# First mixer loop of a hybrid decoder step: GpSimd's state product put behind the decay tables, attention copy and tables put ahead of the gates, mLSTM gate sums in one product

## The reference

```
x = post(0, x, _swiglu(pre(0, x), ...), 0.5)     # FFN
y, st = _mix(pre(1, x), l, prm, past)            # three mixers in parallel
x = post(1, x, y, 1.0)
x = post(2, x, _swiglu(pre(2, x), ...), 0.5)     # FFN
```

## Time and profile before

| | |
|---|---|
| median of three runs | 2043.45 us (2041.63 to 2048.05) |
| profiled execution | 2043.22 us |
| its span | 2041.4 us |
| TensorE busy | 1851.3 us (91%), 12436 records |
| VectorE busy | 965.1 us (47%) |
| ScalarE busy | 720.3 us (35%) |
| GpSimd busy | 81.7 us (4%) |
| transfers | 391.48 MB, mean 192 GB/s |

### The profile page before, as it was taken

One profiled execution on the slowest core, in us unless ns is written; L12 is line 12 of the kernel. 1 busy time (PEld: TensorE's weight loads), 2 busy tenths in 40 slices (PEclk: granted clock), 3 DMA queues, 4 the chain that ended last, 5 costly groups with the idle time before them and its releaser, 6 DMA issues. The chain is left out here.

```text
span 2041.4 us, 33570 instructions
## 1 busy us (share of the span) xinstructions
PE 1851.3 (91%) x12436; PEld 1567.1 (77%) x12436; DVE 965.1 (47%) x1749; ACT 720.3 (35%) x1317; POOL 81.7 (4%) x111
## 2 busy tenths in 40 slices
PE   6999989999987897999969999899999878979997
PEld 4988966776765686998959888667767656869997
DVE  4555425335355534555355553253353644346554
ACT  3554323323321103554345443233233211046552
POOL 0000010000000001000010000100000000010001
PEclk7999989999998998999979999999999888989999
DMA  7777642462348922456547776342641588325561
GB/s 320 279 281 293 252 170 84 167 232 109 134 154 211 272 104 101 166 200 254 226 165 271 299 292 227 146 161 81 237 183 59 165 256 224 110 99 174 213 229 69
DMA packets 87842, 391.48 MB, mean 192 GB/s; under 512 B 14402, under 2 KB 19778, under 8 KB 57410
## 3 DMA queue, kind: packets, MB, share of 16 engines
q1 hardware_dynamic: 72738, 368.24, 50.8%
q10 hardware_dynamic: 15008, 21.95, 2.9%
HBM read 377.32 MB, written 12.83 MB: 191 GB/s over the span
## 5 line engine op out<-in xcount | busy, mean ns | idle before, releaser
L982 DVE TENSOR_TENSOR ring_parts<-ring,pages_parts 128x1024 fp32r<-128x1024 f32 (+1 forms) x272 | 314.3, 1191 | 199.2 <-ACT pages_parts L1539 199.1
L451 PE MATMUL ps<-xn,ring 128*128 128x264 f32 x1664 | 400.0, 401 | 6.1 <-ACT xn L1546 6.1
L490 PE MATMUL ps<-arena_parts,pages_parts 128*128 128x264 f32 x1408 | 361.4, 292 | 23.5 <-DVE xn_parts L1050 21.1
L451 PEld LDWEIGHTS ps<-xn,ring 128*128 128x128 f32 x1664 | 326.9, 199 | 70.0 <-issue 10.4
L491 PE MATMUL ps<-xn_parts,pages_parts 128*128 128x264 f32 x1408 | 357.0, 288 | 0.0
L1539 ACT ACTIVATE pages_parts<-ring 128x1024 fp32r<-128x1024 f32 (+1 forms) x272 | 267.8, 1025 | 179.8 <-DMA ring<-in_w_ffn_in 71.8
L490 PEld LDWEIGHTS ps<-arena_parts,pages_parts 128*128 128x128 f32 x1408 | 271.8, 193 | 44.2 <-issue 43.6
L491 PEld LDWEIGHTS ps<-xn_parts,pages_parts 128*128 128x128 f32 x1408 | 271.2, 193 | 0.0
L495 PE MATMUL ps<-arena_parts,ring_parts 128*128 128x264 f32 x1408 | 196.5, 283 | 0.0
L490 PE MATMUL ps<-big_parts,pages_parts 128*128 128x264 f32 x704 | 177.6, 288 | 6.6 <-DVE gates_parts L996 6.6
L495 PEld LDWEIGHTS ps<-arena_parts,ring_parts 128*128 128x128 f32 x1408 | 181.9, 188 | 0.0
(11 more groups left out here) (312 smaller groups left out, 2039.6 us busy)
## 6 DMA issues: line engine op xcount, KB each, us to landing
ring<-in_w_ffn_in SPq DMA_DIRECT2D x88, 1024.0 KB, 4.9
ring<-in_w_ada SPq DMA_DIRECT2D x32, 1536.0 KB, 6.5
ring<-in_w_a SPq DMA_DIRECT2D x32, 1536.0 KB, 11.1
ring<-in_w_ffn_down SPq DMA_DIRECT2D x32, 1408.0 KB, 6.5
pages<-in_k_pages SPq DMA_DIRECT2D x128, 256.0 KB, 5.0
pages<-in_v_pages SPq DMA_DIRECT2D x128, 256.0 KB, 6.2
ring<-in_w_ada SPq DMA_DIRECT2D x24, 1024.0 KB, 7.2
ring<-in_w_proj SPq DMA_DIRECT2D x8, 1536.0 KB, 9.4
```

The source lines that it names most:

```text
L451: last = mm(ps[:, b, 0:T], tile_of(r, first + k), rhs(k), start=(k == 0), stop=(k == depth - 1))
L490: mm(ps[:, b, 0:T], tile, hi[:, k, :], start=start, stop=False)
L982: v.tensor_tensor(ring_lo[:, r, at * P:(at + n) * P], w, whi[:, place, 0:n * P].bitcast(F32), ALU.subtract)\
```

## The change

- TensorE: the second weight slot's three products are done in the order hi, hq, hf (and ScalarE's destinations follow), and step 2's transposes wait for four copied-out products, not six.
- TensorE: the gate sums are three matmuls with 8 weight columns into M1, not six with 4 into M1 and M2. VectorE adds them in one instruction into `gates8` (8 rows, gi its first four). Behind the loop one matmul with a part of the identity moves rows 4 to 7 to PSUM's VROW bank, from where the bias addition reads them.
- TensorE: the transposes L764 stand ahead of the square sum L761, whose wait goes with it.
- VectorE: the attention copy, the tables and L1252 stand ahead of L1242 and L1243; the gate addition stands behind ql.
- ScalarE: the table's absolute value and exponential stand ahead of the evacuation of slot 4's first product.
- GpSimd: f * S waits for `dlr` as well.

```diff
-                            for n in range(3):
+                            for n in ((0, 1, 2), (2, 0, 1))[k]:
                                 product(r, n * KC, xn_of, KC)
...
-                        pe.wait_ge(S.evac, i * 12 + (before_a + 6 + 4))
+                        pe.wait_ge(S.evac, i * 12 + (before_a + 4 + 4))
...
-                        for g in range(2):
-                            for j in range(3):
-                                last = mm(ps[0:4, M1 + g, 0:T], hp[:, WIF + j * 8 + 4 * g:WIF + j * 8 + 4 * g + 4],
-                                          qkv[:, j, i, :], start=(j == 0), stop=(j == 2))
+                        for j in range(3):
+                            last = mm(ps[0:8, M1, 0:T], hp[:, WIF + j * 8:WIF + j * 8 + 8], qkv[:, j, i, :],
+                                      start=(j == 0), stop=(j == 2))
...
-                        pe.wait_ge(S.osq, i + 1)
-                        mm(ps[:, M2, 0:T], ones, w2, start=True, stop=True).then_inc(S.hss, 1)
                         pe.wait_ge(S.zrow, i + 1)
                         for n in range(4):
                             last = nc.tensor.transpose(ps[:, Z, n * P:(n + 1) * P], rbuf[:, n * P:(n + 1) * P], ident)
                         last.then_inc(S.ztr, 1)
+                        pe.wait_ge(S.osq, i + 1)
+                        mm(ps[:, M2, 0:T], ones, w2, start=True, stop=True).then_inc(S.hss, 1)
...
+                pe.wait_ge(S.gir, HEADS)
+                mm(ps[0:4, VROW, 0:T], ident[0:8, 4:8], gates8[:], start=True, stop=True).then_inc(S.gt, 1)
                 pe.wait_ge(S.dve_it, HEADS + 1)
...
-                    dve.wait_ge(S.sge, i + 1)
-                    link(v.tensor_copy(mo[:, i, :], sgt[:, 1, :]))
-                    link(v.tensor_tensor(sgt[:, 0, :], sgt[:, 0, :], pj[:, HG_, :], ALU.mult))
                     dve.wait_ge(S.av, i + 1)
                     v.tensor_copy(ob[:, i, 0:TP], ps[:, M0, 0:TP]).then_inc(S.obr, 1)
...
-                    dve.wait_ge(S.gt, i + 1)
-                    link(v.tensor_tensor(gi[:], gi[:], ps[0:4, M1, 0:T], ALU.add))
-                    v.tensor_tensor(gf[:], gf[:], ps[0:4, M2, 0:T], ALU.add).then_inc(S.gir, 1)
+                    dve.wait_ge(S.sge, i + 1)
+                    link(v.tensor_copy(mo[:, i, :], sgt[:, 1, :]))
+                    link(v.tensor_tensor(sgt[:, 0, :], sgt[:, 0, :], pj[:, HG_, :], ALU.mult))
                     dve.wait_ge(S.elr, i + 1)
                     v.tensor_tensor(ql, e8, pj[:, HQ_, 0:TP].unsqueeze(1).broadcast_to([P, LEVELS, TP]), ALU.mult)\
                         .then_inc(S.qlr, 1)
+                    dve.wait_ge(S.gt, i + 1)
+                    v.tensor_tensor(gates8[:], gates8[:], ps[0:8, M1, 0:T], ALU.add).then_inc(S.gir, 1)
...
-                link(v.tensor_scalar(gf[:], gf[:], lp4[:, 1:2], None, ALU.add))
-                link(v.tensor_scalar(gi[:], gi[:], lp4[:, 0:1], None, ALU.add))
+                dve.wait_ge(S.gt, HEADS + 1)
+                link(v.tensor_scalar(gf[:], ps[0:4, VROW, 0:T], lp4[:, 1:2], None, ALU.add))
+                link(v.tensor_scalar(gi, gi, lp4[:, 0:1], None, ALU.add))
...
-                    evac(r, before + 2, gates[:, i * 4 + 1, :], exp=True)
                     act.wait_ge(S.dlr, i + 1)
                     link(A(e8, e8, ACT.Abs))
                     A(e8, e8, ACT.Exp, scale=-1.0).then_inc(S.elr, 1)
+                    evac(r, before + 2, gates[:, i * 4 + 1, :], exp=True)
...
                     pool.wait_ge(S.fsr, i + 1)
+                    pool.wait_ge(S.dlr, i + 1)
```

More of the change, by code:

```diff
@@ L235, in build @@
         ot = sb("ot", [P, T])
-        gi = sb("gi", [4, T])
+        gates8 = sb("gates8", [8, T])
+        gi = gates8[0:4, :]
         gf = sb("gf", [4, T])
@@ L1179, in _ @@
                 last.then_inc(S.qmr, 1)
-                link(v.memset(gi[:], 0.0))
-                link(v.memset(gf[:], 0.0))
+                link(v.memset(gates8[:], 0.0))
                 before_a = products.count.n
                 with dve.Fori(0, HEADS) as i, slots.loop(i, HEADS, [3] * 4), products.count.loop(i, HEADS, 12), \
-                        link.loop(i, HEADS, 24):
+                        link.loop(i, HEADS, 23):
                     for k in range(4):
@@ L1679, in _ @@
                     act.dma_start(st8[:], ins.hgrn[layer, i]).then_inc(S.hpar, 16)
-                    dests = [pj[:, SK_, :], pj[:, SV_, :], xp[:, 3:3 + T], pj[:, HQ_, :], pj[:, HF_, :], pj[:, HI_, :],
+                    dests = [pj[:, SK_, :], pj[:, SV_, :], xp[:, 3:3 + T], pj[:, HI_, :], pj[:, HQ_, :], pj[:, HF_, :],
                              pj[:, HG_, :], sgt[:, 1, :], gates[:, i * 4, :]]
```

## The result

The changed kernel took 1997.63 us (median of four runs, 1993.95 to 2006.17) against 2043.03 us: a ratio of 0.9774, 95% interval 0.9752 to 0.9796, so 45 us faster where 51 were forecast (1992). The profiled execution took 1993.95 us, its span is 1992.2.

The account below looks back on a forecast made before the run. TensorE's waits in the first loops, and its clock behind them, were taken to bound the kernel. Gains of 41.4 + 4.2 - 0.3 + 6.5 = 51.8 us from 2043.2 gave 1991.4, stated as 1992 us, range 1985 to 2007.

Parts of the forecast that it names:

- What bounds the kernel: First loops: TensorE is otherwise full, so its waits (2.6 us before L705 in each pass) and its clock count; transfers don't bound.
- Attention copy first: VectorE behind the scan: the attention copy starts 2.29 us earlier, leaving some 0.3 of L705's 2.62 us hole.
- Tables ahead of the evacuation: From the attention copy to L727: L727 at 1429.4 instead of 1434.79, 5.35 us a pass, 4.0 in layer 1's first, 41.4 total.
- The cover for the moved instructions: L1242 and L1243, 2.3 us even when stalled by GpSimd, fit beside ScalarE's 3.85 us table, done 1.1 us before ql.
- The rival of the collision: GpSimd's product holds L1242 and L1243 longer, so ql comes late: 8 to 14 us lost, 2000 to 2006; chance 0.08.
- Halving the gate product: TensorE's gate matmuls before L727: the 1.3 us saved (10.4 in all) lie beside VectorE's chain, so worth nothing by itself.
- Transposes ahead of the sum: Pass's end: four transposes, some 0.9 us, fill TensorE's 0.7 us wait for ScalarE; 6 x 0.7 = 4.2 us.
- Transposes after four evacuations: L675 at the pass's start: the 0.5 us saved becomes wait before L688, so 0; bounds 0 and 3.8 us.
- The clock at the pass's end: Behind L757: two thirds of six 1.63 us stretches at 1.2 GHz go, 6.5 us; bounds 0 and 9.8.
- Outside the loops: The second loops and the FFNs move earlier and keep their length.
- the one in which the half clock stays: Rival: 1.2 GHz stays behind L705 and the pass's end, TensorE is late before L727: 2004.5 us; chance 0.13.
- the one that "frees less": Rival: the attention copy or the key pages keep TensorE waiting 1 to 2 us a pass: 2004 us; chance 0.06.

Follow-up runs that it names:

- e10: Kernel before with only VectorE's new order (attention copy, tables and L1252 ahead of the mLSTM gate's copy and HGRN2 gate's product): 2012.23 us, ratio 0.983.
- e11: Kernel before with one line alone, GpSimd's product waiting for the tables (`dlr`): 2021.69 us, ratio 0.9901.
- e2: Changed kernel with GpSimd's state product no longer waiting for the tables (only that edit undone): 2004.01 us, ratio 0.9803.
- e4: Changed kernel with ScalarE's evacuation of slot 4's first product ahead of the table again (only that edit undone): 2022.24 us, ratio 0.9891.
- e3: Changed kernel with the three gate matmuls done twice, so TensorE's gate work is as long as before the change: 2004.01 us, ratio 0.9794.
- e6: Changed kernel with the square sum ahead of the four transposes again (only that edit undone): 2000.51 us, ratio 0.9766.
- e8: Changed kernel with ScalarE's store issues of k, v and conv_p moved behind its softplus of the attention scores: 1993.05 us, ratio 0.9737.
- e5: Changed kernel with the eight matmuls at the pass's end (L757) streaming 64 equal columns instead of one: 1996.07 us, ratio 0.975.
- e12: Changed kernel with both the 64 columns in the pass's last matmuls and the three stores issued later: 1986.26 us, ratio 0.9715.

## Why the prediction was right, and where its terms were not

- **What bounds the kernel.** Right. The loops shrank by 49.8 us in the profile; counted from the evacuation behind the sixth product, which the earlier transposes don't move, 51.
- **Attention copy first.** 2.29 us a pass forecast, 2.30 measured (10.10 to 7.80). e10 shows that VectorE's order alone does it, e11 that GpSimd's product had been 1.4 us of it. The Trainium skill (SBUF — State Buffer, Who interferes with whom) says that the one of the two that issues first holds the shared port pair for its whole instruction. The runs agree: 0.30 us (e11) and 1.68 (before) for the same copy, 0.41 and 1.47 for a table difference (e2, e10), 0.43 unchanged for the copy out of PSUM (e2).
- **Tables ahead of the evacuation.** The part behind the value product was forecast at 3.06 us in seven passes (5.35 less 2.29) and 1.7 in the first; measured 3.3 and 1.85. With the term above that is 43.3 us instead of 41.4. e4 shows the weight of ScalarE's order: 1.8 us a pass, and another 0.9 through the clock.
- **The cover for the moved instructions.** Its end was right, its inside wrong. I had the mLSTM copy stalled, and it was the multiplication behind it (L1254), since the copy started 0.24 us before GpSimd's product. The 1.1 us of room was a slip too: 3.85 less 2.3 is 1.55, and L1254 ended 1.66 us before ql started. The rival of the collision was priced with the 1.1, so too high.
- **Halving the gate product, "worth nothing by itself".** This step failed. I compared it with a chain that was late by 0.4 us, and did not subtract: of 1.3 us only the 0.6 that TensorE waits before L727 is covered there. And I costed the key pages at nothing although I had them landing 8.8 to 9.2 us after their places were free, with 9 needed. e3: without the halving the pass is 1.3 us longer, 0.56 at L727 and 0.72 at the pages. So the halving was worth the whole of its own time. The sum did not suffer, since TensorE's own arrival was worked out with the halving in it.
- **Transposes ahead of the sum.** 4.2 us forecast. The wait went from 0.7 to 0.2, not to zero, and e6 gives 0.3 us a pass, 1.8 in six: the term was more than twice too large. I had taken the filler, the four transposes, for 0.9 us. That is near what they take at 1.2 GHz (1.06 in the pass of the earlier trace rows); at 2.4 GHz they take 0.64.
- **Transposes after four evacuations.** Zero, as forecast: the wait before the suffix sums grew from 0.3 to 1.0 (0.8 was expected). From L757 to the next suffix sums, the stretch in which the edit lies, e10 without it and e6 with it both take 34.71 us where the clock holds. e8 shows what the wait hangs on: ScalarE's chain, of which the store issues are the first part.
- **The clock at the pass's end.** 6.5 us forecast, four of six ends free at 1.7 us each measured, 6.7. The size is partly luck: no row gave the two thirds, and profiles of kernels with the same order have two to six ends free of six. The reason given, that the wait goes, can't be more than a part. Ends stay at 1.2 GHz without the wait (15 of 42) and are free with it (5 of 30). With 64 columns in the last matmuls, in nearly the same time, all 12 ends of e5 and e12 are at 2.4 GHz, so the one-column matmuls are needed for the fall, as far as two profiles show it. The Trainium skill (TensorE: Matmul & The Clock Gate, Part 1) calls the throttled state the default that activity releases. The trace agrees as far as the stretches at 1.2 GHz stand behind waits and behind the one-column matmuls, and TensorE is full where the clock is back.
- **Outside the loops.** "Keep their length" held for all but the second loops. Together they take 255.6, 255.8 and 255.5 us in the two profiles of the kernel before and in e11, and 256.7 to 262.4 in the two of the changed kernel and 259.2 to 262.6 in the other variants. So some 1 to 7 us are given back there, which is about what the median gained less than the forecast. TensorE waits in them for value pages: 32.7 us in both profiles of the kernel before, 33.9 in e11, and 34.7 to 39.1 in all others, so that wait has a part in it. Its clock is at 1.2 GHz for part of the time in all kernels: 0.88 and 0.84 on average before, 0.84 and 0.87 after. How the rest divides, and why the pages are later there, stays open. No run here changed only the second loop.

None of the rivals came in whole. Of the one in which the half clock stays, two of the six pass ends did, and none of the places behind L705; the page wait, which I had put into the one that "frees less", is there at 0.8 us in all.

## What to carry to other kernels

Before sizing a reorder, write the finishing times of all engines that meet at a wait beside each other: the slack that covers one edit is what another edit uses up, and a transfer that is issued by the step before can be the next to be late by half a microsecond. An elementwise instruction of 0.3 us can be the most expensive line of a pass when GpSimd runs beside it and TensorE stands behind it; one wait on GpSimd was worth 22 us in the kernel before (12 to 28 by the interval). Behind the new order on VectorE the same line was worth 1.05 us a pass, for there GpSimd's product held up only a table difference. Ask of each hole in TensorE what it does to the clock behind it, and of each row of narrow matmuls too.

## What the runs showed of the hardware that was not expected

- Behind the eight pairs of one-column matmuls (1.84 us) TensorE's clock was at 1.2 GHz in 2 of 6 places in each of two profiles of the changed kernel and in 6 of 6 in each of two of the kernel before. With 64 equal columns the same matmuls cost 0.06 us more, and it was so in none of 12 (e5, e12).
- A VectorE instruction with two SBUF inputs was held by GpSimd's product as fully as the plain copy: 0.43 us of multiplication took 2.09.
- A wait of TensorE of 2.5 or 2.6 us can cost more than itself. In e4 the clock behind it was 0.50 in seven of eight passes and the next stretch 0.9 us longer, in the kernel before 1.4, also in seven of eight. Behind waits of 1.2 us (e11, before L705) and 1.7 us (e2, before L727) it was 1.00 in all eight.
